# Four small tiles declared earlier in SBUF, so that eight working tiles start 96 bytes later and three tables 160 bytes later

## The reference

```
y = rmsnorm(x, norm_mix);  q, k, v = split(y @ w_in)      # 16 heads of 64
s = q k^T / 8 + rel_bias[bucket(distance), head]; s = -inf above the diagonal
h = x + softmax(s) v @ w_out
h = h + square(relu(rmsnorm(h, norm_mlp) @ mlp_up)) @ mlp_down     # 4096 hidden
out = rmsnorm(h, final_norm)
```

## Time and profile before

| | |
|---|---|
| median of three runs | 323.28 us (322.73 to 323.43) |
| the profiled execution's own time | 322.73 us |
| its span, first to last instruction | 321.0 us |
| TensorE, matmul | busy 307.3 us, 96% of the span |
| VectorE | busy 205.7 us, 64% |
| ScalarE | busy 160.8 us, 50% |
| mean granted TensorE clock | 0.996 |

### The profile page before, as it was taken

One profiled execution on the slowest core, in us unless ns is written; L12 is line 12 of the kernel. 1 busy time (PEld: TensorE's weight loads), 2 busy tenths in 40 slices (PEclk: granted clock), 3 DMA queues, 4 the chain that ended last, 5 costly groups with the idle time before them and its releaser, 6 DMA issues.

```text
span 321.0 us, 5025 instructions
## 1 busy us (share of the span) xinstructions
PE 307.3 (96%) x1734; PEld 261.7 (82%) x1734; DVE 205.7 (64%) x366; ACT 160.8 (50%) x293; POOL 6.5 (2%) x14
## 2 busy tenths in 40 slices
PE   5699999999999999989999999999999999999992
PEld 2588899898998888988888888888888888888881
DVE  3786675665666667968656854765585477548454
ACT  2584644734834736626543644464364446445322
POOL 2001000000000000000000000000000000000000
PEclk9999999999999999999999999999999999999998
DMA  6999763463454372545665657465655746530003
GB/s 182 358 308 350 264 198 131 131 196 131 135 192 131 133 233 83 208 136 178 184 225 168 225 140 242 150 193 191 190 201 143 249 149 215 158 131 0 0 2 131
DMA packets 36589, 55.90 MB, mean 174 GB/s; under 512 B 1073, under 2 KB 29905, under 8 KB 36578
## 3 DMA queue, kind: packets, MB, share of 16 engines
q1 hardware_dynamic: 35586, 52.50, 50.6%
q0 software_dynamic: 992, 3.25, 3.4%
HBM read 54.67 MB, written 1.07 MB: 174 GB/s over the span
## 4 chain that ended last, share of the span: by engine, by line
PE 89%; DVE 4%; ACT 3%; DMA 2%; issue 1%; SPq 0%; DVEq 0%; ACTq 0%
PE bank L338 31%; PE bank L287 27%; PE bank L288 14%; PE bank L267 3%; PE bank L268 2%; PE bank L269 2%; DMA raw<-in_a_w_in_dram 2%; DVE w_lo L668 2%; PE bank L376 1%; PE bank L306 1%; PE bank L377 1%; PE bank L322 1%; PE bank L321 1%; PE bank L299 1%; PE bank L320 1%; PE bank L297 1%
## 5 line engine op out<-in xcount | busy, mean ns | idle before, releaser
L668 DVE TENSOR_TENSOR w_lo<-raw,w_hi 128x1024 fp32r<-128x1024 f32 x96 | 115.6, 1221 | 63.1 <-ACT w_hi L490 59.8
L287 PE MATMUL bank<-yT,w_hi 128*128 128x512 f32 x368 | 132.0, 400 | 0.0
L490 ACT CAST w_hi<-raw 128x1024 fp32r<-128x1024 f32 x95 | 97.6, 1047 | 53.8 <-PE bank L338 52.9
L288 PE MATMUL bank<-yT,w_lo 128*128 128x256 f32 x368 | 103.2, 280 | 0.0
L287 PEld LDWEIGHTS bank<-yT,w_hi 128*128 128x128 f32 x368 | 69.1, 188 | 16.9 <-DVE w_lo L668 0.6
L338 PE MATMUL bank<-w_hi,hT 128*128 128x512 f32 x256 | 71.8, 390 | 0.0
L288 PEld LDWEIGHTS bank<-yT,w_lo 128*128 128x128 f32 x368 | 69.5, 189 | 0.5
L338 PEld LDWEIGHTS bank<-w_hi,hT 128*128 128x128 f32 x256 | 47.0, 188 | 9.7
L338 PE MATMUL bank<-w_lo,hT 128*128 128x512 f32 x128 | 40.2, 390 | 0.0
L338 PEld LDWEIGHTS bank<-w_lo,hT 128*128 128x128 f32 x128 | 24.0, 188 | 5.2
L551 ACT COPY part<-bank 128x256 f32<-128x256 f32 x30 | 11.2, 373 | 23.3 <-PE bank L288 23.3
(11 more groups left out here) (73 smaller groups left out, 261.5 us busy)
## 6 DMA issues: line engine op xcount, KB each, us to landing
raw<-in_mlp_up_dram SPq DMA_DIRECT2D x16, 1024.0 KB, 5.5
raw<-in_mlp_down_dram SPq DMA_DIRECT2D x16, 1024.0 KB, 4.9
raw<-in_a_w_in_dram SPq DMA_DIRECT2D x11, 1024.0 KB, 6.7
raw<-in_a_w_out_dram SPq DMA_DIRECT2D x4, 1024.0 KB, 5.9
bias_sb<-bias_by_distance POOLq DMA_DIRECT2D x4, 512.0 KB, 5.2
h_sb<-in_x_dram SPq DMA_DIRECT2D x2, 512.0 KB, 5.3
raw<-in_a_w_in_dram SPq DMA_DIRECT2D x2, 512.0 KB, 7.4
out_dram<-y_sb SPq DMA_DIRECT2D x4, 256.0 KB, 2.2
```

What stands on the lines that cost most here:

```text
L287: mm(dst[:], wh[:, k, own], yT[:, k, :, :], start=(k == 0), stop=False, skip_group_check=True)
L288: last = mm(dst[:, 0:T], wl[:, k, own], yT[:, k, HI, :], start=False, stop=(k == KB - 1), skip_group_check=True)
L490: nc.scalar.copy(w_hi[:, slot, part_of], raw[:, slot, part_of]).then_inc(hi_done, 1)
L668: v.tensor_tensor(w_lo[:, slot, own], raw[:, slot, own], f32(w_hi[:, slot, own]), ALU.subtract).then_inc(lo_done, 1)
```

## The change

The declaration of `rel_sb` moves ahead of `onehot_sb`, and those of `negmax`, `rowsum` and `rinv` ahead of `part`. No instruction, wait or transfer is added, removed or moved in order; only the addresses differ.

```diff
         oT = sb("oT", [P, PAIRS, 2, T], F32R)
+        negmax = sb("negmax", [P, 2, 4])
+        rowsum = sb("rowsum", [P, 2, 4])
+        rinv = sb("rinv", [P, 2, 4])
         part = sb("part", [P, 2, T])
...
         ident = sb("ident", [P, P])
+        rel_sb = sb("rel_sb", [BUCKETS, HEADS])
         onehot_sb = sb("onehot_sb", [BUCKETS, BV])
         fill_sb = sb("fill_sb", [HEADS, BV])
         bv_sb = sb("bv_sb", [HEADS, BV])
-        rel_sb = sb("rel_sb", [BUCKETS, HEADS])
-        negmax = sb("negmax", [P, 2, 4])
-        rowsum = sb("rowsum", [P, 2, 4])
-        rinv = sb("rinv", [P, 2, 4])
         stat = sb("stat", [P, 6, 5])
```

## The result

| | before | after |
|---|---|---|
| median | 323.0 us (322.6 to 323.43, 4 runs) | 324.95 us (324.13 to 325.31, 4 runs) |
| ratio of the runs | 1 | 1.0056, 95% interval 1.0032 to 1.0081 |
| profiled execution's span | 321.0 us | 323.0 us |

The forecast was no difference, 323.3 us with a range of 322.6 to 324.6. The measured 324.95 us lies above that range, and the interval of the ratio lies above 1. (The median before is here over four runs.) The page of the kernel after shows where: only TensorE is busy for longer, by 2.2 us.

The account below looks back on a forecast made before the run. The prediction took TensorE's instruction spacing to bound the kernel in three quarters of the time. Its five terms, each 0, summed to no change: the earlier three-run median, 323.28, say 323.3 us, range 322.6 to 324.6.

Parts of the forecast that it names:

- What bounds the kernel: Whole kernel: TensorE busy 307.3 of 321.0 us, so in three quarters of the time only its instruction spacing counts.
- a): TensorE's 384 loads of `hT` as weights in `down`: hidden behind the preceding matmul, 0 us; ends 0 and +4.8 us.
- must become some 90% slower before it shows: Loads of `hT` in `down`: 0.2275 us spacing less at most 0.12 us for a load leaves 0.108 us of cover.
- The prediction's own sign: In `down`: the claim of no cost for `hT` loads is wrong if 24 matmuls take more than 5.5 us.
- The upper end, 4.8 us: Loads of `hT` in `down`: if doubled, 0.0125 us each over 384; among harsh variants given 0.02, total 328.1 us.
- 9 lines for 8: Loads of `hT`: 512 bytes per partition starting half a 64-byte line late touch one more line, 12.5%.
- b): `ident` streaming in 96 transposes: taken as 0; slower rival 1.3 us, harsh form 10.6 us, chance 0.06 including harsh variants.
- c): VectorE and ScalarE accesses to shifted tiles: 0 us, mostly covered; 17 ns per instruction at most, 2.7 us without cover.
- d): `negmax`, `rowsum`, `rinv`, on the path between 103 and 119 us: place within a 64-byte line kept, 0 us.
- e): Transfers of `ident`, tables and `bv_sb`, ahead of the weight landing at 8.71 us: 0, ends -0.03 and +0.2 us.
- The prediction's term of 0.03 us for `ident`: Transfer of `ident`: some 15% more if the 256-byte boundary rule held for the written side.
- Collisions between engines: Rival: shifted `hT` and `part` meet other engines' accesses more or less often; 0.1 to 2.7 us, chance 0.03.

Follow-up runs that it names:

- the measuring kernel: Separate kernel computing nothing of the layer, only matmuls with weight loads at shifted operand starts; 512 columns took 226.7 ns at equal starts.

## Why the prediction was wrong, step by step

- *What bounds the kernel.* Right: TensorE without idle time, so its spacing is the time. That was the reason to look at its operands, and a) was the right place.
- *a) Loads of `hT`.* This is the step that failed: the overlap, taken for complete. It said that a load has 0.108 us of cover and "must become some 90% slower before it shows". That counts the load as an occupant of a path of its own, beside a stream that it doesn't touch. The runs showed that the two operands aren't independent: the load's own duration stayed 188 ns, and the spacing of `down` rose by 6.3 ns, 2.4 us in all. It depends on the distance between the two starts, 226.7 ns at 0 and 234.3 at 96 bytes with nothing else at work. By the records, a longer load isn't what cost the time, so its cover didn't help. The prediction's own sign fired: 24 matmuls of `down` took 5.61 us, over its mark of 5.5. The upper end, 4.8 us, held the 2.4 us measured, but only by luck: it was reached by a wrong road (a load twice as long), given 0.02 at the most, and left out of the range.
- "9 lines for 8" in the same part, and the question whether a start is a multiple of 64, were the wrong variable. No run shows a line of 64 bytes. Every tile off a multiple of 64 costs nothing measurable (1.0005); `hT` on a multiple of 64 but at distance 64 or 128 costs as much or nearly as much.
- *b) The moving `ident`,* the rival on the slow side: nothing. Six transposes took 0.66 us, and the ratio was 1.0011 with `ident` still shifted. *c) ScalarE and VectorE:* nothing; the products with `gain` stayed at 684 ns in the median, L787 at 418. *d)* nothing. *e)* the landing moved from 8.71 to 8.44 us, and between 7.34 and 9.06 in the profiled runs of the other layouts, without an order; that is a single execution each. The prediction's term of 0.03 us for `ident` is too small to be seen in it.
- *Collisions between engines.* Something did disturb TensorE, but not another engine. The evidence against it, equal durations of the loads, couldn't have shown it: those durations are equal after the change too.
- The trace of before held a hint that was not used. A matmul of 512 columns in `up` holds TensorE for 235.8 ns on average until the next starts (worked out from the starts in the MLP), and one in `down` for 227.8: the same width, other operands, another spacing. Had that been asked about, "what sets the spacing above the bare stream" would have become an unknown with a price of some 8 ns on 480 matmuls, 3.8 us on either side of nothing, and the range would have been wider both ways.

## What to carry to other kernels

Where TensorE is never idle and loads weights for every matmul, the SBUF addresses of the loaded and of the moving operand are part of its speed, through their distance, for 512 columns modulo 256 bytes: here up to 7.6 ns in 227 per matmul. That was measured with float32 data in the kernel's rounded form (`F32R`) alone. Before reordering declarations, check whether a small tile comes to stand between the two; a padding tile is a cheap thing to try, and gave 0.7% here. Judge it by the distance between starts, since the durations of the load don't move.

## What the runs showed of the hardware

- Weight loads and the moving stream are not independent. With 512 columns: 226.7 ns at distance 0, 228.9 at 192 bytes, 231.8 to 234.3 at all other distances tried (loaded start 16 to 160 or 384 bytes later, moving start 16, 32, 96 or 128 bytes later); back at 227.0 to 227.4 at 256 bytes; the same to 0.1 ns with VectorE and ScalarE idle or busy. The Trainium skill (SBUF — State Buffer, "Who interferes with whom") gives TensorE two independent read ports and has it wait for nobody. That TensorE waits for nobody else agrees with these runs as far as VectorE and ScalarE go (the 0.1 ns); the independence of the two doesn't (226.7 against 234.3 ns), and the measurement decides.
- 256 columns want another distance: 113.3 ns at 64 bytes, 119.8 at 0, and 117.3 to 118.5 at the three others tried.
- Groups of alternating widths fall into a fixed rhythm that work before them selects: 340 or 350 ns per pair in one and the same layout. In the kernel after, every third block of `up` ran in a faster rhythm than before, which hid 0.37 us of the loss.
- Not tried: what in the chip makes the 256 bytes, and whether a busy DMA shifts these figures. DMA ran at half its share in the layer (0.53 in the MLP), and there `down` came within 1.1 ns of the measuring kernel's figures, which had no transfers, at all five distances from 0 to 128 bytes.
